# Two PSUM banks for transposed weights and three for scores in the first layer's attention, in place of three and two

## The reference, cut to what matters

```
h = [16 meta tokens ; 1024 tokens]                      # 1040 x 1024
layer 0: q,k,v,g of 4 A heads and 8 B heads = h @ w_in
  A head: s_m = q_m k_m^T / 8 - slope*|distance|, chunk mask, softmax, m = 0, 1
          w = p_0 - lambda * p_1 ;  o = w @ v ; RMS norm ; * silu(g)
  B head: z = q k^T / 8 ; w = stick-breaking weights (a product scan over sigmoid(-z))
          o = w @ v ; * silu(g)
  h1 = LayerNorm(alpha*h + concat(A, B) @ w_out)
layer 1: 8 latent-attention heads (low-rank q and kv, rotary part), softmax, gate, w_out, LayerNorm
```

## Time and profile before

| | |
|---|---|
| median of 3 runs (lowest to highest) | 1565.58 us (1564.21 to 1566.16) |
| profiled execution: its own time, its span | 1564.86 us, 1563.1 us |
| TensorE busy (matmul) | 1420.8 us, 91% of the span |
| VectorE, ScalarE, GpSimd busy | 850.1, 557.2, 525.2 us |
| mean granted clock of TensorE | 0.953 of 2.4 GHz |

### The profile page before, as it was taken

One profiled execution on the slowest core, in us unless ns is written; L12 is line 12 of the kernel. 1 busy time (PEld: TensorE's weight loads), 2 busy tenths in 40 slices (PEclk: granted clock), 3 DMA queues, 4 the chain that ended last, 5 costly groups with the idle time before them and its releaser, 6 DMA issues.

```text
span 1563.1 us, 22642 instructions
## 1 busy us (share of the span) xinstructions
PE 1420.8 (91%) x8604; PEld 1289.7 (83%) x8604; DVE 850.1 (54%) x1941; ACT 557.2 (36%) x1267; POOL 525.2 (34%) x426
## 2 busy tenths in 40 slices
PE   6999898989899999997899998998998989898896
PEld 6898797979788988986688997897887979887685
DVE  4666758585576746566244213424666656656243
ACT  3444344443544535253011004333344444434111
POOL 3213121212223042227544332532223222235553
PEclk9999998999999999997899999998999989989898
DMA  5000100000110010103433211111101111112541
GB/s 189 28 28 28 41 28 29 27 28 28 41 35 21 21 48 18 38 18 88 142 132 109 95 55 54 56 62 52 44 29 34 45 38 35 42 41 83 167 148 68
DMA packets 50796, 90.39 MB, mean 58 GB/s; under 512 B 4720, under 2 KB 33648, under 8 KB 50560
## 3 DMA queue, kind: packets, MB, share of 16 engines
q1 hardware_dynamic: 48384, 80.55, 16.0%
q10 hardware_dynamic: 2304, 8.39, 1.3%
HBM read 67.82 MB, written 21.10 MB: 57 GB/s over the span
## 4 chain that ended last, share of the span: by engine, by line
PE 44%; POOL 4%; DVE 4%; ACT 2%; issue 2%; DMA 1%; POOLq 0%; SPq 0%; ACTq 0%; DVEq 0%
PE bank L1553 17%; PE bank L1703 12%; PE bank L1625 7%; PE bank L1679 5%; PE bank L1649 2%; POOL big L873 2%; POOL big L872 1%; ACT rtmp L1079 1%; DVE qpe L1313 1%; PE bank L1576 1%; DVE qpe L1309 1%; DVE rtmp L1259 1%; DMA wraw<-y_scratch 1%; DVE rtmp L1257 0%; DVE rtmp L1258 0%
## 5 line engine op out<-in xcount | busy, mean ns | idle before, releaser
L1553 PE MATMUL bank<-big,wsp 128*128 128x344 f32 (+1 forms) x3024 | 583.5, 336 | 49.0 <-DVE qpe L1313 26.4
L1553 PEld LDWEIGHTS bank<-big,wsp 128*128 128x128 f32 x3024 | 495.3, 194 | 60.2 <-issue 22.1
L872 POOL TENSOR_SCALAR wsp<-wraw 128x1024 fp32r<-128x1024 f32 (+2 forms) x92 | 83.7, 910 | 495.4 <-PE bank L1553 416.9
L1679 PE MATMUL bank<-ring,vtok 128*128 128x256 f32 (+3 forms) x1276 | 206.1, 299 | 10.2 <-DVE ot L1438 4.8
L1411 DVE TENSOR_TENSOR ring<-bank,ring 16x256 fp32r<-16x256 f32 (+3 forms) x292 | 154.9, 550 | 109.7 <-ACT ring L1139 107.1
L1703 PE MATMUL bank<-big,wsp 128*128 128x512 f32 x816 | 195.7, 401 | 18.0 <-POOL wsp L873 18.0
L1679 PEld LDWEIGHTS bank<-ring,vtok 128*128 128x128 f32 (+1 forms) x1276 | 178.7, 200 | 35.4 <-issue 22.8
L1139 ACT ACTIVATE ring<-bank 16x256 fp32r<-16x256 f32 (+3 forms) x292 | 136.2, 487 | 191.5 <-PE bank L1649 116.4
L1703 PEld LDWEIGHTS bank<-big,wsp 128*128 128x128 f32 x816 | 155.7, 192 | 54.5 <-POOL wsp L873 18.3
L873 POOL TENSOR_TENSOR wsp<-wraw,wsp 128x1024 fp32r<-128x1024 f32 (+2 forms) x92 | 185.9, 2020 | 7.7
L1553 PE MATMUL bank<-h1t,wsp 128*128 128x344 f32 (+1 forms) x1080 | 174.7, 322 | 3.7 <-DVE kpe L1304 2.2
(11 more groups left out here) (115 smaller groups left out, 1493.9 us busy)
## 6 DMA issues: line engine op xcount, KB each, us to landing
wraw<-in_w SPq DMA_DIRECT2D x47, 512.0 KB, 3.5
wraw<-y_scratch SPq DMA_DIRECT2D x17, 512.0 KB, 5.3
wraw<-in_wo SPq DMA_DIRECT2D x16, 512.0 KB, 3.6
y_scratch<-ot SPq DMA_DIRECT2D x48, 128.0 KB, 1.8
gate_scratch<-gtmp SPq DMA_DIRECT2D x8, 520.0 KB, 2.9
gate<-gate_scratch SPq DMA_DIRECT2D x8, 520.0 KB, 3.6
xres<-in_x SPq DMA_DIRECT2D x8, 512.0 KB, 6.1
h_scratch<-res ACTq DMA_DIRECT2D x8, 512.0 KB, 4.7
```

The costliest lines, as they stand in the source:

```text
L872: pool.wait_ge(S["pool_step"], tick(nc.gpsimd.tensor_scalar(hi, raw, 1.0, 1.0, ALU.mult, ALU.mult)))
L1553: ins = mm(dst, wsp[:, SLOT[kind, u], a, k, :], rhs[:, b, k0 + k, c0:c0 + w], start=(k == 0 and a == 0 and b == 0), stop=last)
L1679: ins = mm(PO[:, o0:o0 + wide], l, B["ring"][0:rows, r % NRING, part, at:at + wide], start=(k == 0 and tile == turns[0][0] and part == 0 a ...
```

## The change

The bank lists of layer 0 are changed: bank 4 goes from turns to scores. Since `weave` is given the lengths of these lists, the orders of all engines in layer 0's attention are laid out anew. Layer 1's lists stay. No instruction is added or removed.

```
-SCORE_BANKS = ((2, 3), (2, 3, 4))
-TURN_BANKS = ((4, 5, 6), (5, 6), (5, 6))
+SCORE_BANKS = ((2, 3, 4), (2, 3, 4))
+TURN_BANKS = ((5, 6), (5, 6), (5, 6))
```

## The result

The changed kernel takes 1543.2 us (median of 4, 1539.94 to 1544.79) against 1565.87 us: ratio 0.9853, 95% interval 0.9833 to 0.9872, 22.7 us less. A second set gave 0.9848 (0.9821 to 0.9875). I had forecast 1562.2 us and a range of 1555 to 1572 us: the direction was right, the size far off. The kernel before was run again beside every experiment; its medians there lie between 1564.2 and 1565.5 us, and the ratios of the experiments are against those runs (a ratio can differ from the quotient of two medians by up to 0.1%).

The account below looks back on a forecast made before the run. TensorE was taken to bound layer 0's attention (93% busy). Score waits gain 7.05 us (1.85 and 5.20), turns cost 3.7, all else counts 0: -3.35 us on the median 1565.58 gives 1562.2 us, range 1555 to 1572 us.

Parts of the forecast that it names:

- What bounds the kernel: Layer 0's attention, 45 to 711 us: TensorE bounds it, 93% busy; only its idle time and clock losses are worth anything.
- Third bank for scores, norm stretches: Score waits at the norm in units 1 to 3: of 5.80 us, 1.85 us come back; the holes move.
- Third bank for scores, the other waits: Three score waits outside the norm stretches (0.90, 1.32, 2.98 us), two behind a sigmoid on ScalarE: all 5.20 us come back.
- Third turn bank: Layer 0's turns on two banks instead of three: more waits for a bank, costing 3.7 us.
- The rest behind the last projection: Attention left after 711 us: some 2 us later, under the slack of 2.65 us, so cost 0.
- Order laid out anew: Layer 0's new instruction order: the same total work, counted 0, with some 4 us to either side.
- Clock: Lower clock in and behind two norm holes, worth 4.4 us: counted as nothing, since the holes would stay in length.
- Slower, by the turns at the end: Last B unit behind 711 us: turns wait behind scans, 3.9 us slower, about 1569.5 us; chance 0.28.
- All waits come back: Layer 0: 11.0 us of score waits and 4.4 us of clock return, turns cost 3.7; about 1553.9 us; chance 0.10.
- The range: Whole kernel's time: 1555 us, just short of the fastest rival, to 1572 us, near the slower one's price.

Follow-up runs that it names:

- e1: The kernel before with bank 4 taken from layer 0's turns and given to nobody, order laid out anew: 1564.25 us, ratio 0.9993.
- e2: The changed kernel's banks (three for scores, two for turns) with the order of e1, laid out for two score banks: 1560.2 us, ratio 0.9966.
- e12: The changed kernel with bank 4 as a third bank for turns once layer 0's last score is out: 1542.59 us, ratio 0.9856.
- e17: The changed kernel with its layout assuming 1700 ns for GpSimd's query copies in place of 1400 in layer 0: 1548.92 us, ratio 0.9882.
- e13: The changed kernel with its layout assuming 2000 ns for GpSimd's query copies in place of 1400 in layer 0: 1568.01 us, ratio 1.0015.

## Why the prediction was wrong, point by point

- *What bounds the kernel*: right. Time was only to be had from TensorE's idle time, its clock, and work moved behind the last projection, and the table's remainder bears that out.
- *Third bank for scores, norm stretches*: right in its mechanism. The holes there moved: in units 1 to 3 they sum to 17.8 us before and 16.6 us after, 1.2 us back where I took 1.85 us. With the order kept (e1 to e2) not even that came back. The Trainium skill's rule ("Perfetto Trace Analysis", section Optimization Strategy: a gap that recurs on the engine that should be saturated can mean too few buffers) would have had 5.80 us come back; the measurement disagrees, as VectorE was full behind the gap.
- *Third bank for scores, the other waits*: mostly wrong. Of 5.20 us, 1.7 came back: L1625 behind L1108 still waits 3.5 us of 4.3, and the 0.90 us is gone. I had ScalarE "only late with that one piece", and no bank mends what makes it late: between two sigmoids stands the norm's square root of the same moment, and ScalarE loads a table on each change, 1.28 us each, in the kernel before (at 415.66 and 417.52 us) as in the changed one (the lines below this list). The rows' sum looks better than it is: 7.5 us of score waits went, where I had 7.05, but the norm's grew by 4.6 us (L1570 from 6.5 to 10.4 us, L1553 behind L1288 from 5.5 to 6.2). e2 puts the third bank with the order kept at 4.1 us, most of it the clock (above).
- *Third turn bank*: cost 3.7 us expected, nothing measured in e1 (-0.07%, interval within 0.2%), though there with a new order too. The waits themselves did come, 3.1 us before 711 us in place of 0.4, so layer 1's row of no such waits didn't hold here; other waits went (query copies 11.2 to 7.7 us). In the changed kernel they are 1.1 us. The 3.26 us that I took for the longest scan wasn't: one at 458.76 us of the kernel before took 4.46 us.
- *The rest behind the last projection*: 0 expected, 2.3 us measured, and by another way than the one I priced: a third bank for turns gains nothing there (e12), and GpSimd was busy 2.1 us longer, because one gate was held by a scan. I had given over 40 us there as a sign of the slower rival, together with L946 waiting for L1438; the 41.4 us came without that wait.
- *Order laid out anew*: this is the step that failed. "I count 0, with some 4 us to either side." Measured: about 17 us of the 22.7 (e2 against the changed kernel, with the same banks). I took a new order to be the same work with small waits moved about. The runs show that each layout has its own set of waits of 1 to 3 us on other engines; between e2 and the changed kernel they differ by 10 us of idle time and 13.5 us of running at 1.2 GHz. Against the kernel before went the query copies' 6.3 us, the weight split's 3.2 us, and the 3.0 us of products behind the evacuation of `ot` (L1423); the first two are in the earlier trace rows.
- *Clock*: 0 counted, because the norm's holes would stay. They stayed, and the stretches at 1.2 GHz in and behind them went only from 23.9 to 20.5 us. But the holes that went elsewhere took slow running with them: 12.9 us less in all, 6.4 us of time.
- *The rivals*: none named the layout as a cause of tens of us. "Slower, by the turns at the end" has no support. "All waits come back" had the right sign of the clock's part but put the cause in the wrong place, and its 1553.9 us lay 11 us above the measured time.
- *The range*: what was missing was one more source of spread. Ten layouts of the two bank lists span 1543 to 1568 us; my 4 us for it should have been 12 us to either side.

The wait of 2.96 us that the third bank left, with ScalarE's tables before it (the changed kernel, ScalarE then TensorE):

```profile
404.55 1.28 ACT L1071 ACT_TABLE_LOAD   x1
...
406.41 1.28 ACT L1108 ACT_TABLE_LOAD   x1
...
408.29 1.22 PE L1625 MATMUL bank<-kst,qst 128*128 128x456 f32 x4 [2.96 <-ACT tb L1108]
```

What stays open: whether three score banks make a fast layout likelier (four of five against one of five is no proof), what either bank is worth by itself on an order of its own, and which property of a layout one could have read ahead of time to know on which side it falls.

## What to carry to other kernels

Where the order of all engines is laid out by a planner, a change of one of its inputs is two changes, the resource and a new draw of the order, and the second can be the larger, here by four times. Where it can be done, keep the order and change only the resource (e1 against e2). And before the gain is put down to the resource, move an unrelated assumption of the planner on both kernels, several times and by different amounts: two such moves agreed here, a third by 21% (1700 ns) agreed too, and by 43% (2000 ns) it reversed the result in both. And when forecasting such a change, give the new order a spread of its own. Ten layouts here spread over 25 us, with 44 to 62 us of idle time and 22 to 72 us at the lower clock up to the last projection.

## What the runs showed of the hardware

- The same wait of 1.9 us at the same place was followed by 2.4 GHz in one kernel and by 13.7 us at 1.2 GHz in the other (e17, e13). With one and the same order, e1 ran 6.8 us at 1.2 GHz from 45.8 us on and e2 didn't, behind a wait of 0.51 us in both. A row of a wait doesn't tell what the clock does behind it.
- A scan of 1040 on VectorE and an instruction on GpSimd take turns where they meet: the second to begin makes no headway until the first ends. The scan goes from 2.30 us alone to at most 4.55 us and ends 2.18 us after GpSimd's instruction; a split's first half (L872) goes from 1.05 to at most 3.06 us in the changed kernel, a gate from 0.73 to 2.74 us. None of it shows as a wait in the rows, only as a longer instruction.
- ScalarE loaded a table at each change between the square root and the sigmoid, 1.28 us each, and TensorE's wait behind two of them wasn't shortened by one more score bank (2.98 us in e1, 2.96 in e2, with the same order).
